# Attention on one core: the exponentials become the moving operand, in two column halves, and the row sums come from ones and from pair sums made on GpSimd

## The reference

```python
def one(qblk):
    s = jnp.einsum('bqkgd,bskd->bkgqs', qblk, k).astype(jnp.float32) * scale
    p = jax.nn.softmax(s, axis=-1).astype(v.dtype)
    return jnp.einsum('bkgqs,bskd->bqkgd', p, v)
```

## Time and profile before

| what | value |
| --- | --- |
| three runs | 2376.93, 2380.0, 2381.06 us, median 2380.0 |
| span of the profiled execution | 2375.2 us |
| what lies around the span against the median | 4.8 us |
| TensorE busy | 97% of the span |
| main part of the attention (8 tiles), within the span | 1156.15 to 1401.01 us |

### The profile page before, as it was taken

How to read it: one execution, slowest core, us unless ns; L and a number is a source line. 1 busy time by engine, 2 the same in 40 slices (tenths; PEclk the granted TensorE clock), 3 DMA queues, 4 the chain that set the end, 5 groups by cost and what they waited for, 6 DMA issues and landing times. The chain is left out here.

```text
span 2375.2 us, 44414 instructions
## 1 busy us (share of the span) xinstructions
PE 2301.3 (97%) x17959; PEld 2126.0 (90%) x17959; DVE 1388.8 (58%) x2203; ACT 810.0 (34%) x1398; POOL 224.3 (9%) x244
## 2 busy tenths in 40 slices
PE   6999999999999899999999999998999999999997
PEld 5887779999999889998999989877999999998886
DVE  4331266533554467665455546768676676667877
ACT  5321132213333233223344444325222223234444
POOL 0000000001110011112211101000121121120001
PEclk9999999999999999999999999999999999999999
DMA  6324632236452532214100228421222232259534
GB/s 279 120 84 182 224 111 107 101 135 202 157 173 85 196 107 90 80 67 158 44 18 13 88 107 311 159 91 62 78 105 91 73 109 91 73 177 273 131 100 124
DMA packets 126864, 295.40 MB, mean 124 GB/s; under 512 B 19808, under 2 KB 63280, under 8 KB 117376
## 3 DMA queue, kind: packets, MB, share of 16 engines
q1 hardware_dynamic: 93360, 236.31, 29.7%
q10 hardware_dynamic: 29392, 41.82, 4.8%
q0 software_dynamic: 3968, 15.21, 1.7%
HBM read 207.83 MB, written 85.53 MB: 124 GB/s over the span
## 5 line engine op out<-in xcount | busy, mean ns | idle before, releaser
L62 PE MATMUL ps<-prj_w,h_hi 128*128 128x512 f32 (+1 forms) x864 | 255.4, 380 | 4.1 <-DVE h_lo L755 4.1
L62 PE MATMUL ps<-h_hi,fill_whi 128*128 128x384 f32 x672 | 235.6, 351 | 4.7 <-ACT fill_st L1119 2.4
L62 PE MATMUL ps<-h_lo,fill_whi 128*128 128x384 f32 x672 | 226.5, 337 | 3.8 <-issue 3.8
L62 PE MATMUL ps<-wt 128*128 128x320 f32 (+2 forms) x1046 | 227.2, 327 | 2.3 <-DVE merged L3205 1.3
L62 PE MATMUL ps<-h_hi,fill_wlo 128*128 128x384 f32 x672 | 226.6, 337 | 0.1
L62 PE MATMUL ps<-ys,mergedr 128*128 128x256 f32 (+1 forms) x1056 | 219.6, 297 | 0.4 <-issue 0.4
L62 PE MATMUL ps<-zb,mergedr 128*128 128x320 f32 (+2 forms) x764 | 200.1, 326 | 4.9 <-issue 2.7
L62 PE MATMUL ps<-zb,wt 128*128 128x384 f32 (+3 forms) x758 | 200.2, 325 | 0.0
L62 PEld LDWEIGHTS ps<-prj_w,h_hi 128*128 128x128 f32 x864 | 158.3, 191 | 42.8 <-issue 10.6
L62 PEld LDWEIGHTS ps<-wt 128*128 128x128 f32 x1046 | 179.6, 189 | 16.7 <-issue 2.6
L62 PEld LDWEIGHTS ps<-ys,mergedr 128*128 128x128 f32 x1056 | 174.5, 190 | 0.7 <-issue 0.7
(11 more groups left out here) (502 smaller groups left out, 4675.5 us busy)
## 6 DMA issues: line engine op xcount, KB each, us to landing
wraw<-in_w_ffn_in SPq DMA_DIRECT2D x22, 1024.0 KB, 5.3
prj_raw<-in_w_ada SPq DMA_DIRECT2D x16, 1024.0 KB, 6.0
fill_raw<-in_w_fill SPq DMA_DIRECT2D x30, 512.0 KB, 4.4
wtf<-a_dram SPq DMA_DIRECT2D x55, 256.0 KB, 2.7
bg_dram<-fill_st ACTq DMA_DIRECT2D x72, 192.0 KB, 2.0
xf<-bg_dram POOLq DMA_DIRECT2D x24, 576.0 KB, 7.1
tok_dram<-prj_tst ACTq DMA_DIRECT2D x45, 256.0 KB, 2.1
prj_raw<-in_w_tok SPq DMA_DIRECT2D x10, 1024.0 KB, 6.9
```

The lines of the kernel that those rows point to most:

```text
L62: mm = pe.matmul(out, lhs[a], rhs[b], start=first and n == 0, stop=last and n == 2, skip_group_check=onto)
```

## The change

`values` swaps its operands. The values (128 keys x 64 columns, one head group each) are stationary, in the left or the right half of the array's columns (`kv * HD`), and the exponentials of that head group (512 columns) move. One key tile thus needs 2 matmuls for both head groups in place of 8. The output comes with head columns on the partitions, as it is to be stored, so the four transposes of `output` go. The row sums no longer come from a 65th column: a stationary block of 128 x 32 ones, at one of four column positions for each head, takes the exponentials in 8 matmuls of 128 columns (`add`). Key tiles 0 to 5 are first summed in pairs on GpSimd (`pair_up`, 128 x 1024), tiles 6 to 8 go alone, so a query tile has 6 such sums. VectorE takes the reciprocal of 128 x 256 sums (`inverted`), 8 more matmuls (`spread_sums`) spread it over the partitions, and VectorE multiplies (`normed`). The loops are written out, both head groups go in one step, all eight `shift_scores` of the next tile stand in this one, the score banks are two in place of three, the exponentials have a ring of five buffers, and the output's DMAs are issued by SyncE.

```diff
             def values(i, j):
+                n = NT * i + j
+                pe.wait_ge(sem["ex"], 2 * n + 2)
                 if j == 0:
-                    pe.wait_ge(sem["on"], n + 1)
+                    if i:
+                        pe.wait_ge(sem["evict"], i)
...
+                for kv in range(KV):
+                    mm = pe.matmul(ps[kv * HD:kv * HD + HD, OB, :], va[:, j, kv, 0:HD], pt[n % RING][:, kv, :],
+                                   start=j == 0, stop=j == NT - 1)
-                for a in range(G):
-                    mm = pe.matmul(ps[:, OB, a * H1:a * H1 + H1], pt[j % 3][:, a * P:a * P + P], va[:, j, kv, :],
-                                   start=j == 0 and a == 0, stop=j == NT - 1 and a == G - 1)
+            def add(x, first, last):
+                for kv in range(KV):
+                    for a in range(G):
+                        mm = pe.matmul(ps[32 * a:32 * a + 32, SB, kv * P:kv * P + P], ones[:], x[:, kv, a * P:a * P + P],
+                                       start=first and kv == 0, stop=last and kv == KV - 1)
+                mm.then_inc(sem["sums"], 1)
+            def spread_sums(i):
+                pe.wait_ge(sem["rc"], i + 1)
...
+                for a in range(G):
+                    for kv in range(KV):
+                        mm = pe.matmul(ps[kv * HD:kv * HD + HD, PT, a * P:a * P + P], spread[:, a, :], rs[:, kv, :],
+                                       start=True, stop=True)
+            def tile(i):
+                more = i < LAST
+                for j in range(NT):
+                    for kv in range(KV):
+                        scores(i, kv, j)
+                    if more and j < 2:
+                        queries(i + 1, j)
+                    if i and j == 2:
+                        spread_sums(i - 1)
+                    if more and j == 5:
+                        shifts(i + 1, 0)
+                    if more and 1 <= j < NT - 1:
+                        shift_scores(i + 1, j - 1)
+                    if j:
+                        values(i, j - 1)
+                    if j in PAIR_AT:
+                        pair_sums(i, PAIR_AT.index(j))
+                    if j >= 7:
+                        sums(i, j - 1)
+                    if more and j == NT - 2:
+                        shift_scores(i + 1, AH - 1)
+                if more:
+                    shifts(i + 1, 1)
+                values(i, NT - 1)
+                sums(i, NT - 1)
...
+            branch_tile(pe, ps, 0, [g.wt[:, 2 * n, :] for n in range(2)], g.ys0, thirds=range(0, 2))
+            spread_sums(LAST)
+            branch_tile(pe, ps, 0, [g.wt[:, 2 * n, :] for n in range(2)], g.ys0, thirds=range(2, 3))
@@ gpsimd
+            def pair_up(i, p):
+                u = PAIRS * i + p
+                gp.wait_ge(sem["ex"], 2 * (NT * i + 2 * p + 2))
...
+                gp.tensor_tensor(pair[u % 2][:], pt[a][:], pt[b][:], ALU.add).then_inc(sem["paired"], 1)
@@ vector
+            def inverted(i):
+                v.wait_ge(sem["sums"], (NT - PAIRS) * (i + 1))
...
+                v.reciprocal(rs[:].rearrange("p k n -> p (k n)"), ps[:, SB, 0:KV * P]).then_inc(sem["rc"], 1)
```

More of the change, by code:

```diff
@@ L1897, in attention @@
         kn = ph.sb("kn", [P, NT, KV, HD])
+        with ExitStack() as later:
+            over = lambda name, shape, dt=F32: later.enter_context(nc.sbuf_tensor(f"att_{name}", shape, dt))
+            pt = [over(f"pt{i}", [P, KV, G * P]) for i in range(RING)]
+            pair = [over(f"pair{i}", [P, KV, G * P]) for i in range(2)]
         k2 = ph.sb("k2", [P, NT, KV, HD])
@@ L2170, in _, with shifts, scores @@
-            group(7, 1, False)
-            output(use(7, 3), 8)
+            def shifts(i, kv):
+                pe.wait_ge(sem["nm"], AH * i + G * kv + G)
+                pe.wait_ge(sem["pte"], turn(i, 2 + kv))
+                if kv == 0 and i >= 2:
+                    pe.wait_ge(sem["norm"], i - 1)
+                turn_shifts(pe, kv, PT).then_inc(sem["ptm"], 1)
+            def scores(i, kv, j):
+                u = 2 * NT * i + 2 * j + kv
+                if u >= 2:
+                    pe.wait_ge(sem["ex"], u - 1)
+                if j == 0:
+                    pe.wait_ge(sem["pte"], turn(i, 2 + kv) + 1)
+                out, at = ps[:, ST + kv, :], slice(j * P, j * P + P)
+                pe.matmul(out, kt[0][:, kv, at], qt[i % 2][kv][:], start=True, stop=False)
+                pe.matmul(out, kt[1][0:H1, kv, at], qm[i % 2][kv][0:H1, :], start=False, stop=True).then_inc(sem["s2"], 1)
@@ new lines, in _ @@
+            queries(0, 0)
+            shift_scores(0, 0)
+            queries(0, 1)
+            branch(range(20, 21), (0, 2))
+            shift_scores(0, 1)
+            pe.wait_ge(sem["pte"], 2)
+            for t in range(4):
+                mm = pe.transpose(ps[:, PT, t * P:t * P + P], y[:, 2 * t:2 * t + 2, :].rearrange("p h d -> p (h d)"), g.ident[:])
+            mm.then_inc(sem["ptm"], 1)
+            branch(range(20, 21), (2, 4))
+            for u in (21, 22, 23):
+                shift_scores(0, 2 * u - 40)
+                if u == 23:
+                    shifts(0, 0)
+                branch(range(u, u + 1), (0, 2))
+                shift_scores(0, 2 * u - 39)
+                branch(range(u, u + 1), (2, 4))
@@ L2172, in _ @@
+            shifts(0, 1)
+            for i in range(LAST + 1):
+                tile(i)
             pe.wait_ge(sem["b1lo"], 5)
-            branch_tile(pe, ps, 0, [g.wt[:, 2 * n, :] for n in range(2)], g.ys0)
+            branch_tile(pe, ps, 0, [g.wt[:, 2 * n, :] for n in range(2)], g.ys0, thirds=range(0, 2))
+            spread_sums(LAST)
+            branch_tile(pe, ps, 0, [g.wt[:, 2 * n, :] for n in range(2)], g.ys0, thirds=range(2, 3))
         @block.scalar
@@ L2245, in group, with queries @@
[L2245 to L2260 removed]
+            def queries(i, kv):
+                act.wait_ge(sem["ptm"], turn(i, kv) + 1)
+                act.activation(qt[i % 2][kv][:], ps[:, PT, :], ACT.Copy).then_inc(sem["pte"], 1)
@@ new lines, in output, with tile @@
+            def output(i):
+                act.wait_ge(sem["pv"], NT * i + NT)
+                if i:
+                    act.wait_ge(sem[f"yout{(i + 1) % 2}"], 16 * ((i - 1) // 2 + 1))
+                act.activation(yt[(i + 1) % 2][:].rearrange("p t n -> p (t n)"), ps[:, OB, :], ACT.Copy).then_inc(sem["evict"], 1)
+            def tile(i):
+                more = i < LAST
+                for j in range(NT):
+                    exponentials(i, j)
+                    if more and j < 2:
+                        queries(i + 1, j)
+                    if more and j == 5:
+                        shifts(i + 1, 0)
+                    if not more and j < 6:
+                        ahead(j)
+                if more:
+                    shifts(i + 1, 1)
+                output(i)
```

325 lines of the change are left out of this document (159 added, 166 removed).

## The result

| | before | changed |
| --- | --- | --- |
| median, us (20 runs each) | 2377.4 | 2381.3 |
| ratio, 95% interval | | 1.002, 1.0013 to 1.0027 |
| span of the profiled execution, us | 2375.2 | 2379.4 |

The changed kernel is slower by 3 to 6 us. I had forecast 2374.3 us and faster: the time lies in the range (2366 to 2384), the sign is wrong. The forecast was a difference of -5.7 us from the median of three runs, 2380.0; with 20 runs that median is 2377.4, so the difference to set beside -5.7 is +3.9. One run of the changed kernel took 2647 us at a granted clock of 0.81, where the others had 0.99, and is left out of the ratio.

A forecast was written before the change was run, and what follows sets the result against it. TensorE was taken to bound the attention tiles. Lead-in +6.2, seven tiles -9.2, last tile -4.8, spreading in the branch tile +1.2 and barrier +0.9 gave -5.7 us from 2380.0: 2374.3 us, range 2366 to 2384.

The forecast's parts named there:

- Who could be late in a tile: Check of other engines in a tile: maximum needs 2.1 of 2.6 us, later query's norm costs nothing to 0.1 us.
- seven tiles: First seven query tiles: 206.8 us in all, 9.2 less than before.
- My GpSimd line: GpSimd's work in a tile: 16 us, power then pair 1, pair sum 3.3 us, allowed up to 4.5.
- lead-in: Stretch before the tiles: 21.6 us, 6.2 more, of which 3.2 are TensorE's waits as eight maxima pass through.
- barrier: End of the phase: last output leaves later, so the barrier waits 0.9 us longer.
- last tile: Last query tile: 24.1 us against 28.86, 4.8 less.
- a tile with nothing late: TensorE's time for one query tile: 29.7 us against 30.86, 1.2 less.
- a visit to `values` in all: TensorE's stretch in `values`: two passes, 0.853 us, plus 0.34 for getting in and out, 1.19; nine visits a tile.
- change from 64 to 32 columns: Column width change between `values` and row sums, four places a tile: 0.13 us each, an estimate, 0.5 a tile.
- Rivals 2 and 5: 2: form changes cheaper than 0.34 us, 2363 or 2369, chance 0.17. 5: halves not side by side, 2442, chance 0.05.
- Rival 4: GpSimd late in the tiles: slower from pair sums near 5 us, at 5.5 +15 us, 2395; chance 0.08.
- Rival 3: Lead-in waits of half a us let the clock fall again: -2 to +2 us, 2380; chance 0.20.

The follow-up runs named there:

- e7: Changed kernel with GpSimd's first pair sum of a tile put ahead of the power of the squared norms: median 2369.8 us, ratio to before 0.9963.
- e1: Changed kernel without VectorE's copy of the rotation table, GpSimd reading the table in place: median 2380.7 us, ratio to before 1.0016.
- e3: Changed kernel with each GpSimd pair sum cut into four instructions of 128x256: median 2373.9 us, ratio to before 0.9989.
- e4: Kernel before, plus a GpSimd addition of 128x1024 behind each power and an unused VectorE reduction ahead of the table copy: median 2379.4 us, ratio 1.0011.
- e5: Changed kernel without pair sums, TensorE summing all nine key tiles singly: median 2388.1 us, ratio to before 1.0042.
- e11: e9 with VectorE's copy of the rotation table left out too, GpSimd reading it in place: median 2367.2 us, ratio to before 0.996.
- e8: e7 with the last spreading of inverse sums one third of the branch tile earlier: median 2368.6 us, ratio to before 0.9965.
- e9: e8 with lead-in scores of heads 3, 5, 7 in a second PSUM bank set and the next query split after the last maximum: 2368.3 us, ratio 0.9962.
- e10: e7 with the lead-in change of e9, without the earlier last spreading: median 2368.2 us, ratio to before 0.9965.
- e8b: The kernel of e8 run again, unchanged: median 2369.9 us, ratio to before 0.9975.

## Why the prediction was wrong

The step that failed is in "Who could be late in a tile": "The maximum ... must be out before the next `shift_scores`, a step later: 0.52 + 1.36 + 0.2 = 2.1 of 2.6", and for the norm that stands between the first two, "Nothing to 0.1 us." It summed VectorE's work at the durations of before. By those the copy and the product of the norm cost 0.23 + 0.68 us; with the pair sum beside it the copy alone takes 1.87 us, and 2.39 in the first tile. The maximum is then late by 1.1 us of TensorE's time in each of five tiles and by 1.8 in the first, where the clock falls behind the wait. Against e7 that is 1.4 us in each of the five and 3.1 in the first (1.55 more of wait, the rest the clock), 10 us of the 10.8 by which the seven tiles missed. My GpSimd line even had the order of time that makes the collision (power, then pair 1), but asked only whether GpSimd would be late, not whom it would hold. e1, e3, e4, e5 and e7 show the cause: move the pair sum away, and the tiles take what I had worked out.

By stages the forecast was -5.7 us and the traces have +5.8. The 11.5 between them are 10.8 in the seven tiles, 0.9 in the lead-in, 0.1 at the barrier and -0.3 in the last tile.

Point by point:

| step | forecast, us | measured, us |
| --- | --- | --- |
| a tile with nothing late | 29.7 | 29.70 |
| a visit to `values` in all | 1.19 | 1.2 |
| `values`, from its start to the next score's | 0.853 + in and out | 1.01 |
| change from 64 to 32 columns | 0.13, bounds 0 and 0.34 | 0.14 |
| pair sum | 3.3 | 2.38 |
| reciprocal of 256 columns | 0.4 to 4 | 1.76 |
| lead-in | 21.6 | 22.47 |
| seven tiles | 206.8 | 217.59; e7 207.58 |
| last tile | 24.1 | 23.78 |
| spreading in the branch tile | +1.2 | +1.2 |
| barrier | +0.9 | +1.0 |

- The sum for the seven tiles has a slip: 7 x 29.7 - 1.2 + 0.3 is 207.0 and not 206.8. e7's tiles lie 0.6 above that, all in the first, which took 29.34 us for 28.8; 0.45 of it are two waits, for the query's second part (0.21) and for a maximum (0.24).
- TensorE's own costs were right to 0.1 us a tile: the 0.34 us of getting into and out of a tiled stretch from two other phases, halves side by side, and the change of width between them. Rivals 2 and 5 are out.
- The lead-in is 0.9 us longer than forecast, its waits for maxima as described (0.41, 0.47, 0.38, 0.38 and 1.13 us). One head follows the other by 2.25 us, where I had put 2.1, and the last, long wait is VectorE's split, which I had at 0.35 and which costs TensorE 0.75.
- Rival 4 had the right engine and the wrong victim. GpSimd was never late: a pair sum took 2.38 us, not over 4.5, and TensorE waits for `att_pair` nowhere. It held VectorE.
- Rival 3 came nearest to the measured time (2380), but by luck. More was given back in the lead-in, 0.9 us, but by the maxima; its clock fell once, behind waits of 1.41 and 0.69 us as before (granted 0.92, before 0.89), and not again behind the waits of half a us. The other fall, in the first tile, stands behind the 1.79 us wait for the held maximum; in e7, which has no such wait, the tile ran at 1.00.
- With the copy's wait cured and all else as changed (e7), the kernel is 7.7 us faster than before by the medians (2377.5 in that comparison) and 3.0 by the stage, where its lead-in had 1.1 us more of the clock's dip than the changed kernel's; forecast -5.7. The 4.7 us between the two ways of counting stay open; the profiled run of e7 was the slowest of its five (2373.0 us for a median of 2369.8). So the prediction's sum for the tiles describes a kernel that the change was one line away from. The fastest tried, e11, is 0.4% under before.

## What to carry to other kernels

When work moves to GpSimd, don't ask only if GpSimd keeps up. Lay its long instructions over VectorE's fp32 copies and two-operand instructions, and count each of these that can start behind one as ending no sooner than it (the copy ended 0.09 us after the addition, the product 0.55). If such a pair stands ahead of something that TensorE waits for, start the GpSimd instruction earlier, or cut it into pieces; here the first cost the tiles nothing (29.71 us) and the second 0.3 us each (30.00). And a median of five runs does not show 1 or 2 us here: a stage's length in the trace does, if the clock's dips in it are looked at too.

## What the runs showed that I had not expected

- An fp32 copy of 128 x 128 took 0.23 us alone, 1.86 to 2.39 behind a GpSimd addition of 128 x 1024, and 1.31 when a reduction had used up the first part. With four GpSimd pieces of 0.72 us the hold was at most one piece long (copy 0.75 in the first tile and 0.23 in the others, product 1.24).
- The hold goes both ways: a GpSimd piece of 0.72 us took 1.18 behind VectorE's product of 0.68.
- VectorE's subtractions for the next branch (`ahead`) are stretched as well in the last tile, 1901 ns for 1350 and 3375 for 2282, and in e5, without pair sums, they are back at 1354 and 2292. The last tile is no longer for it (23.78 us, forecast 24.1).
- A 128 x 1024 addition takes GpSimd 2.38 us, with both operands the same 1.89 (e4).
- The same lead-in ran at a granted clock of 0.92 (22.46 us, e8) and of 0.86 (23.60, e7), and the one with two sets of banks at 0.91 (19.15, e9) and 1.00 (17.87, e10). The dip lies in the first 6 branch matmuls behind 1.41 and 0.69 us of idle time, which take 2.27 us in e9 and 1.32 in e10. So 1.1 and 1.3 us of the differences between these stages are the clock's and not the kernels'. In the two profiles of one kernel, e8 and e8b, the stages agree to 0.1 us.
